# Two stacked transformer blocks on one core: the biases of the first modulation on ScalarE, constants through TensorE, eight scalings in three portions

## The reference, cut to what matters

```python
def first_block(x, c, norm1_w, norm2_w, w_ada, b_ada, w_in, ...):
    mod = jax.nn.silu(c) @ w_ada + b_ada
    shift1, scale1, gate1, shift2, scale2, gate2 = [m[:, None, :] for m in jnp.split(mod, 6, axis=-1)]
    h = rms_norm(x, norm1_w) * (1.0 + scale1) + shift1
    proj = h @ w_in
    q, k, v, cb, cc, cx, iq, ik, iw = jnp.split(proj, offs, axis=-1)
```

## Time and profile before

| what | value |
|---|---|
| median of three runs | 1210.69 us |
| the profiled execution, its own time | 1205.73 us |
| its span, first to last instruction | 1204.0 us |
| mean granted TensorE clock | 0.968 |
| PE busy | 1062.5 us, 88% |
| DVE busy | 846.8 us, 70% |
| ACT busy | 430.6 us, 36% |
| Pool busy | 315.5 us, 26% |

### The profile page before, as it was taken

The page is one execution under the profiler, slowest core; times in us unless marked ns, Lnnn a source line. Parts: engine busy times, 40 slices in busy tenths (PEclk is TensorE's granted clock), DMA queues, the critical chain, the costliest instruction groups (busy, mean ns, idle before and its releaser), DMA issues.

```text
span 1204.0 us, 18995 instructions
## 1 busy us (share of the span) xinstructions
PE 1062.5 (88%) x7646; PEld 995.5 (83%) x7646; DVE 846.8 (70%) x1787; ACT 430.6 (36%) x900; POOL 315.5 (26%) x317
## 2 busy tenths in 40 slices
PE   5999996979988988787888878788999999999997
PEld 4998995878988888787878877788899888899886
DVE  5999989665666676667676766656764768755776
ACT  3554732122123212221222122212457554476552
POOL 2472005233343334333333433333000000300000
PEclk9999999989999999989988998899999999999999
DMA  9955478999999999999999999999854565454550
GB/s 338 404 223 197 171 280 325 422 420 420 421 421 420 422 421 420 421 420 422 420 421 420 421 420 421 421 421 421 359 187 164 209 207 179 162 188 175 175 175 35
DMA packets 60375, 390.88 MB, mean 325 GB/s; under 512 B 6784, under 2 KB 8832, under 8 KB 16512
## 3 DMA queue, kind: packets, MB, share of 16 engines
q0 software_dynamic: 36864, 268.45, 53.7%
q1 hardware_dynamic: 21808, 120.10, 27.0%
q10 hardware_dynamic: 1616, 1.12, 0.4%
HBM read 388.60 MB, written 1.05 MB: 324 GB/s over the span
## 4 chain that ended last, share of the span: by engine, by line
PE 54%; DMA 35%; DVE 6%; ACT 2%; issue 1%; POOL 1%; DVEq 0%; ACTq 0%
DMA low_pairs<-in_peer_uv,work 24%; PE aux L1421 13%; DMA rows<-in_peer_uv,work 9%; PE pj L1464 5%; PE pj L1466 5%; PE pj L1465 5%; PE pj L1207 5%; PE pj L1208 5%; PE pj L1209 5%; PE aux L1400 3%; DVE low_pairs L1872 1%; PE aux L1277 1%; PE aux L1349 1%; ACT work L1067 1%; POOL rows L841 1%
## 5 line engine op out<-in xcount | busy, mean ns | idle before, releaser
L1421 PE MATMUL aux<-work,low_pairs 128*128 128x128 f32 x2304 | 282.6, 286 | 59.4 <-ACT work L1067 56.9
L1421 PEld LDWEIGHTS aux<-work,low_pairs 128*128 128x128 f32 x2304 | 275.8, 201 | 65.9 <-ACT work L1067 62.8
L1421 PE MATMUL aux<-work,rows 128*128 128x128 f32 x1792 | 222.8, 288 | 50.4 <-ACT work L1067 43.7
L1421 PEld LDWEIGHTS aux<-work,rows 128*128 128x128 f32 x1792 | 217.1, 203 | 55.9 <-ACT work L1067 48.8
L841 POOL DMA_INDIRECT low_pairs<-in_peer_uv,work x144 | 135.7, 942 | 223.5 <-PE aux L1421 220.4
L655 DVE TENSOR_TENSOR wlo<-wring,whi 128x1024 fp32r<-128x1024 f32 x100 | 121.2, 1235 | 88.3 <-ACT whi L649 87.7
L841 POOL DMA_INDIRECT rows<-in_peer_uv,work x112 | 109.1, 974 | 241.3 <-PE aux L1421 167.1
L1207 PE MATMUL pj<-xh,whi 128*128 128x256 f32 x512 | 146.4, 286 | 3.4 <-DVE wlo L589 2.7
L1062 ACT ACTIVATE work<-work 128x4 f32<-128x4 f32 (+2 forms) x71 | 14.7, 207 | 372.6 <-DVE work L1872 372.6
L1208 PE MATMUL pj<-xl,whi 128*128 128x256 f32 x512 | 144.9, 283 | 0.0
L1209 PE MATMUL pj<-xh,wlo 128*128 128x256 f32 x512 | 144.9, 283 | 0.0
(11 more groups left out here) (269 smaller groups left out, 1529.6 us busy)
## 6 DMA issues: line engine op xcount, KB each, us to landing
wring<-in_w SPq DMA_DIRECT2D x79, 1024.0 KB, 4.8
rows<-in_w_ada SPq DMA_DIRECT2D x40, 512.0 KB, 6.7
low_pairs<-in_w_ada SPq DMA_DIRECT2D x1, 4096.0 KB, 13.4
low_pairs<-in_peer_uv,work POOLq DMA_INDIRECT x144
work<-in_late_rows SPq DMA_DIRECT2D x2, 1024.0 KB, 8.0
xT<-in_gate_rows SPq DMA_DIRECT2D x2, 1024.0 KB, 7.1
rows<-in_norm_rows SPq DMA_DIRECT2D x2, 1024.0 KB, 6.8
rows<-in_peer_uv,work POOLq DMA_INDIRECT x112
```

The costliest lines, as they stand in the source:

```text
L1421: ins = mm(peer_sum[t][:, c * P:(c + 1) * P], pair(n)[:, D + c * P:D + (c + 1) * P], diag[:, n % PICKS, :], start=(n % (EXPERT_HEADS * PIC ...
```

## The change

Four places change.

1. **ACT in Pool's place.** Pool's sixteen small instructions (L817, L819) go. ACT first adds 1 to the eight columns of the scale's bias at once (new tile `scale_bias`); this stands before the root's table is loaded, and waits for `cols`. Then, for each chunk, ACT adds the bias to the scale column and to the shift column itself, right before it applies them.
2. **Constants on PE.** Twelve matmuls of `ident` by `blk` (128 columns), whose result nobody reads, stand ahead of the sums of squares; `WARM` gets the number 12 in front, and the three counts that were there stay.
3. **Smaller portions on DVE.** `scale_h` takes chunks 0 and 1, then 2 to 4, then 5 to 7, in place of 0 to 3 and 4 to 7, with the dots of chunk 1 behind the first portion and those of chunk 2 behind the second.
4. The semaphore `mod_ready` counts one more (that of `scale_bias`).

```diff
-WARM = (5, 2, 2)
+WARM = (12, 5, 2, 2)
@@
+        scale_bias = sb("scale_bias", [P, KC])
@@ Pool
-            pool.wait_ge(cols_loaded, 16)
-            for c in range(KC):
-                pool.wait_ge(ada_used, 2 * c + 2)
-                pool.tensor_scalar(gain[:, c:c + 1], mod[:, KC + c:KC + c + 1], cols[:, B_ADA + KC + c:B_ADA + KC + c + 1], 1.0,
-                                   ALU.add, ALU.add).then_inc(mod_ready, 1)
-                pool.tensor_tensor(mod[:, c:c + 1], mod[:, c:c + 1], cols[:, B_ADA + c:B_ADA + c + 1], ALU.add).then_inc(mod_ready, 1)
@@ ACT
-            act.wait_ge(const_ready, 2)
+            act.wait_ge(const_ready, 3)
+            act.wait_ge(cols_loaded, 16)
+            nc.scalar.activation(scale_bias[:, :], cols[:, B_ADA + KC:B_ADA + 2 * KC], ACT.Identity, bias=ones[:, 0:1]).then_inc(mod_ready, 1)
             nc.scalar.activation(warm[:, :], eps[:, 0:1], ACT.Sqrt)
+            act.wait_ge(mod_ready, 1)
             act.wait_ge(x_loaded, 16)
@@
             for c in range(KC):
+                act.wait_ge(ada_used, 2 * c + 2)
+                nc.scalar.activation(gain[:, c:c + 1], mod[:, KC + c:KC + c + 1], ACT.Identity, bias=scale_bias[:, c:c + 1]).then_inc(mod_ready, 1)
+                nc.scalar.activation(mod[:, c:c + 1], mod[:, c:c + 1], ACT.Identity, bias=cols[:, B_ADA + c:B_ADA + c + 1]).then_inc(mod_ready, 1)
                 act.wait_ge(h_scaled, c + 1)
-                act.wait_ge(mod_ready, 2 * c + 2)
+                act.wait_ge(mod_ready, 2 * c + 3)
@@ PE
             pe.wait_ge(const_ready, 7)
+            for _ in range(WARM[0]):
+                mm(aux[:, 1, 0:P], ident[:, :], blk[:, :], start=True, stop=True)
@@
-            warm_up(WARM[0])
+            warm_up(WARM[1])
...
@@ DVE
-            scale_h(0, 4)
+            scale_h(0, 2)
             first_dots(1)
-            scale_h(4, KC)
-            for c in range(2, KC):
+            scale_h(2, 5)
+            first_dots(2)
+            scale_h(5, KC)
+            for c in range(3, KC):
                 first_dots(c)
```

More of the change, by code:

```diff
@@ L1286, in first_products @@
                         ins.then_inc(proj, 2)
-            warm_up(WARM[0])
+            warm_up(WARM[1])
             first_products(0, 0)
             first_products(0, 1)
-            warm_up(WARM[1])
+            warm_up(WARM[2])
             first_products(1, 0)
             first_products(1, 1)
-            warm_up(WARM[2])
+            warm_up(WARM[3])
             first_products(0, 2)
```

## The result

The changed kernel takes 1211.08 us (median of 20 runs, 1209.02 to 1218.06), the kernel before, run beside it, 1208.59 us (20 runs, 1206.4 to 1210.91). The ratio is 1.0031 with an interval of 1.0019 to 1.0042: slower by 0.3%, about 3.7 us; the medians are only 2.5 us apart, since five long runs weigh in the ratio, which goes by the means. The profiled execution took 1210.83 us, its span is 1209.0 against 1204.0. So the sign was forecast, and the size (7.3 us) was twice too large by the ratio and three times by the medians. Of the 20 runs 15 lie between 1209 and 1213.2 and five between 1217 and 1218.1; the profile is one of the first group.

The account below looks back on a forecast made before the run. DVE's list was taken to bound the kernel up to 118 us. Scoring 6.5 later, 3.2 more behind it, 2.2 and 0.2 less: 7.3 us later, 1210.69 + 7.3 = 1218.0 us; range 1209.0 to 1220.5.

Parts of the forecast that it names:

- Part 1: Opening, root: squares start 0.9 us later, but constants speed PE's sums to 3.6 us, ending 1.6 us earlier at 13.9.
- the dearer switch of tables: ACT before the root: a table switch of about 2.66 us, not 1.28, giving about 1218.6 us in all.
- a rival at 0.12: Opening on PE: constants do not lift the clock, sums take 6.2 us; 8.8 us later, 1219.5 us, chance 0.12.
- Part 2: DVE's opening: earlier scaling and dots, limited by tile transfers, so DVE gains 2.0 us, bounds 1.4 and 2.0.
- Part 3: ACT doing Pool's columns frees PE: first products end at 40.9 in place of 45.6, a gain of 4.7 us.
- The lead of PE on DVE: After the opening: PE gains 2.7 us more than DVE, so Pool's pieces come earlier against DVE's list.
- Part 4: DVE's scoring and after: Pool's earlier pieces hold DVE's short instructions, 2.2 us each; sum 7.3 us later.
- so all nine pieces fall into the scoring in place of five: DVE's scoring: nine Pool pieces overlap it, so it ends at 75.8 in place of 69.3, 6.5 us later.
- 3.2 more: Behind DVE's top-k: the pair at L1707 and the two behind it meet three Pool pieces, costing 3.2 us more.
- the 2.2 regained at the first multiply: DVE's first L1717: free of Pool, it takes 1.29 us in place of 3.46, 2.2 us less.
- one or two pieces more, not four: DVE's scoring: same collision with 0.5 us margin, 2.0 less and 2.2 to 4.4 more; 1212.5 us, chance 0.10.
- its neighbour's threshold: Faster rival: with Pool's lead under about 2.0 us DVE's gain passes on; gain 2.2, 1208.5 us, chance 0.17.

Follow-up runs that it names:

- the four extra warm-ups: Four more PE warm-ups ahead of the third unit's first products, on the changed kernel: 1206.71 us, ratio 0.9992 to the kernel before.
- the parts alone: One part each on the kernel before: ACT in Pool's place 1217.89 us (1.0063), twelve constants 1208.01 us (0.9991), smaller portions 1205.36 us (0.9981).
- the moved instructions: Two comparisons and two masks moved from ahead of DVE's reciprocals to behind the second normalising multiply, on the changed kernel: 1208.45 us, ratio 1.0001.

## Why the prediction was right and wrong

**Part 1 failed.** "I take the fast rate for the sums: 8 x 0.45 = 3.6, end 13.9." The constants end at 7.63, ACT's wait for `cols` keeps PE idle 3.29 us, the clock falls back, and the sums take 5.16 and end at 16.1, 2.2 us later than forecast. Of this 0.6 is the later `cols`; the table load took 1.28 us, and the instruction behind it started 0.02 us after its end, so the dearer switch of tables that the prediction names did not show. I had put this case down as a rival at 0.12, from the longest gap that rows showed without a slow start (2.00 us), though part 1 itself makes a gap of three: 7.3 to 10.3. In the profiles of the runs with constants, PE idle for 0.2 to 1.7 us behind them kept the upper level (the sums take 3.72 us in all five), after 2.4 to 3.8 us it did not (5.2 to 6.2 us in all seven). By the Trainium skill ("TensorE: Matmul & The Clock Gate", Part 1), the array is throttled again when idle, and these traces agree. That rival's price was wrong too: 8.8 us, with the same nine pieces as the forecast, where 3.7 were measured. The two parts of the change work against each other here: ACT's wait for `cols` makes the gap in which the constants are lost.

**Part 2**: its gain of 2.0 us was 0. In the change the last dot ends at 39.24, after 38.71 before, its tile waited for (0.32). With an early root it is 1.4 (24 constants) and 1.6 (constants alone), inside the bounds given.

**Part 3**: ACT's columns do free PE. Forecast 4.7 earlier, measured 2.45 (43.15), the root being 2.2 later than forecast; 4.2 with 24 constants. The lead of PE on DVE, 2.7 in the forecast, was 2.4 minus 0.8, so 1.7 us at the scoring.

**Part 4, the mechanism was right, its size was not.** DVE's short instructions and Pool's pieces take turns, a lead of Pool's costs DVE 2.15 us for each piece that falls into the scoring, and a piece more behind the top-k moves all that follows: shown by the four extra warm-ups, by the parts alone and by the moved instructions. **The step that failed** is "so all nine pieces fall into the scoring in place of five": there were seven, as pieces 10 and 11 came just behind its end. The count rests on the lead of 2.7 us, and that on the root of part 1: with the lead of 1.7 the scoring is over when piece 10 starts, and with 24 constants and the early root nine pieces do fall, piece 3 over the last dot and eight over the scoring. Of "3.2 more" at the pair and the masks 0.9 was paid; the 2.2 regained at the first multiply were 1.9. The sum was +7.5 at normed q and k, and is +2.5. The rival "one or two pieces more, not four" at 1212.5, to which I gave 0.10, describes what happened; and its neighbour's threshold (a lead under 2.0 us leaves it at five) was wrong, since a lead of 1.7 cost two pieces.

**What was missing** is how much turns on half a microsecond. Piece 3 ahead of the scoring by 0.23 us (both profiles of the change) or by 0.75 to 0.85 decides between seven and eight held, and by the two groups of runs the latter costs some 7 us. A chain of collisions that is forecast one after another, each as certain, ought to have been given as a share of runs: the forecast's own case needed the clock to stay up and the scoring to reach piece 10, and with the clock up (24 constants) four runs of eleven were that long.

**The last 1.5 us** between piece 20 and the first gather were not in the prediction, which let the end move as piece 20 does. The granted clock shows them. These are the stretches from 120 to 130 us, before and after:

```profile
120.00:130.00 10.00, 10.00 (x86) 10.00 (x85) 9.27 (x28) 9.97 (x27) 1.35 (x2) 1.00 0.76 283
...
120.00:130.00 10.00, 8.34 (x57) 8.34 (x58) 9.93 (x33) 9.49 (x36) 1.33 (x2) 0.83 0.41 132
```

The gap before L1331 has its price too (the clock reads 0.70 from 100 to 110 us, and L1331 takes 6.32 us in place of 4.07), but PE makes it good by waiting less for piece 20. Behind piece 20 it cannot. The seventeen profiles fall into two sets: in nine, the one of before and the second of the change among them, the clock reads 1.00 in the 12 us from piece 20 on, and the first gather comes 70.7 to 70.8 us after piece 20; in eight, the first of the change among them, it reads 0.86 to 0.88, and the gather comes 72.0 to 72.3 us after. Each of the eight has PE idle for 2.4 to 4.5 us just before, but so have three of the nine, by 2.73 us. It is not peculiar to the change: constants with portions, which are no slower than before, show it as well.

## What to carry to other kernels

Before taking small work off one engine to free another, ask what the delay was holding apart: here holds of one to two microseconds on single columns kept PE and Pool's pieces behind DVE's scoring, and the cheap repair was to slow PE by 1.6 us or to move four short instructions, either of which brought the change back to the time of before. Where two engines take turns, count the short instructions that fall under long ones and compare the starts of both; where the count hangs on half a microsecond of lead, expect two groups of run times and give each a chance. Work that is meant to lift the clock has to reach up to what it is to speed up, and an edit of the same change that delays the latter can undo it.

## What the runs showed of the hardware

- **One engine's instruction waits for the other's whole one.** A DVE instruction of 0.2 to 0.5 us takes 2.4 to 2.7 beside a Pool piece of 2.4. The fourteen at L1693 and L1698 take 15.45 us before and 17.56 after, with six of them held in place of five. The Trainium skill ("SBUF — State Buffer", "SBUF: two separate sides") has Pool and DVE take the shared port pair as a lock, whole instructions at a time, with the DVE instructions that have two SBUF inputs or run in a two-port mode; the traces agree: MAX8, its match and replace, and the reciprocal, with one input each, run at their usual length beside the pieces. The masks at L1715 have one input, and one of them is held all the same (two take 2.60 us in the change and 0.41 before, where no piece lies over them). That fits a two-port mode, but no run took the mode away, so it stays a reading.
- The number held goes in steps with the start of piece 3 against that of the scoring: three where the piece comes 3.8 us later, five where 0.6 to 2.0 later (six profiles), seven where 0.1 to 0.6 ahead (four), eight where 0.75 ahead or more (four), and never six. It is not so where Pool is made to wait: seven with the piece 1.5 us later (two profiles), since the pieces behind it close up.
- The hold goes both ways: Pool's column of one value took 2.26 us beside dots, and in the run with 24 constants piece 3 began 0.07 us ahead of a dot, and the dot took 3.42 us in place of 1.22.
- The length of a gap does not by itself say whether the clock falls. Behind constants it fell after 2.39 us and more; among the chunks' products the ten records took 2.43 us, the upper level's time, behind gaps of 2.00 before and of 2.48 to 2.54 with the portions; ahead of piece 20 gaps of 2.73 left it up in three profiles and not in two others.
